# A hybrid decoder step on one core: key copies, gated-row copies, sample exponentials and the scores of two narrow steps moved

## What is computed

```python
def diff_attn_core(q, k, v, qpos, kpos, rel_bias, lam):
    s = jnp.einsum('bqhmd,bkhmd->bhmqk', q, k2) * (QK_HEAD_DIM ** -0.5)
    dist = qpos[:, None] - kpos[None, :]
    s = jnp.where(dist >= 0, s + bias[None, :, None], NEG_INF)
    p = jax.nn.softmax(s, axis=-1)
    a = p[:, :, 0] - lam * p[:, :, 1]
    return jnp.einsum('bhqk,bkhd->bqhd', a, v)
# prompt: causal over its own 1024 keys; sample: over 8 cached pages and its own 8 keys
# o_b = rmsnorm(attention output per head); o_a = u * (tril(W) LayerNorm(v) + b)
# mix = concat(o_b, o_a) @ w_out; x = x + rmsnorm(mix); then ConvFFN: w_up, conv 3, silu(g) * u, w_down
```

## Time and profile before

| | us |
|---|---|
| median of three runs | 1390.12 |
| the profiled execution | 1389.97 |
| its span | 1388.2 |
| TensorE busy | 1360.4 (98%) |
| VectorE busy | 700.8 (50%) |
| ScalarE busy | 460.8 (33%) |
| GpSimd busy | 169.9 (12%) |

### The profile page before, as it was taken

One profiled execution on the slowest core, in us unless ns is written; L12 is line 12 of the kernel. 1 busy time (PEld: TensorE's weight loads), 2 busy tenths in 40 slices (PEclk: granted clock), 3 DMA queues, 4 the chain that ended last, 5 costly groups with the idle time before them and its releaser, 6 DMA issues.

```text
span 1388.2 us, 22368 instructions
## 1 busy us (share of the span) xinstructions
PE 1360.4 (98%) x8646; PEld 1222.2 (88%) x8646; DVE 700.8 (50%) x1169; ACT 460.8 (33%) x780; POOL 169.9 (12%) x322
## 2 busy tenths in 40 slices
PE   7999999989999999999999999999999999999997
PEld 6999999956667788899898989898989898999986
DVE  5333412166778565454546463636454545364555
ACT  5321012055657543343131313231323232322332
POOL 2254000021222221120000000000000000000003
PEclk9999999999999999999999999999999999999999
DMA  7202123256664624132020111111110202020117
GB/s 264 63 31 65 31 69 106 73 175 183 198 192 159 214 90 136 46 106 76 16 76 15 60 30 60 30 60 30 44 46 17 74 15 76 15 67 23 46 31 133
DMA packets 93290, 112.65 MB, mean 81 GB/s; under 512 B 6429, under 2 KB 65222, under 8 KB 93222
## 3 DMA queue, kind: packets, MB, share of 16 engines
q1 hardware_dynamic: 89845, 103.60, 23.7%
q0 software_dynamic: 1136, 4.06, 1.8%
q10 hardware_dynamic: 2240, 4.06, 0.8%
HBM read 96.76 MB, written 14.69 MB: 80 GB/s over the span
## 4 chain that ended last, share of the span: by engine, by line
PE 92%; DVE 2%; issue 2%; ACT 1%; POOL 1%; DMA 1%; SPq 0%; ACTq 0%; DVEq 0%; POOLq 0%
PE PS L2271 37%; PE PS L1996 17%; PE PS L2335 16%; PE PS L2214 7%; PE PS L2082 2%; PE PS L2044 2%; PE PS L2350 2%; PE PS L2365 2%; PE PS L2105 2%; PE PS L2151 1%; PE PS L2128 1%; PE PS L2070 1%; PE PS L1982 1%; PE PS L2206 1%; DMA x_in<-in_x_prompt_dram 1%
## 5 line engine op out<-in xcount | busy, mean ns | idle before, releaser
L2271 PE MATMUL PS<-act_lo,wu_hi 128*128 128x364 f32 (+1 forms) x1056 | 346.4, 328 | 0.0
L2271 PE MATMUL PS<-act_hi,wu_hi 128*128 128x364 f32 (+1 forms) x1056 | 346.0, 328 | 0.2 <-DVE wu_lo L1807 0.2
L2271 PE MATMUL PS<-act_hi,wu_lo 128*128 128x364 f32 (+1 forms) x1056 | 346.0, 328 | 0.0
L2271 PEld LDWEIGHTS PS<-act_hi,wu_hi 128*128 128x128 f32 x1056 | 198.5, 188 | 1.0 <-DVE wu_lo L1807 0.5
L2271 PEld LDWEIGHTS PS<-act_lo,wu_hi 128*128 128x128 f32 x1056 | 198.1, 188 | 0.4
L2271 PEld LDWEIGHTS PS<-act_hi,wu_lo 128*128 128x128 f32 x1056 | 198.4, 188 | 0.0
L1793 DVE TENSOR_TENSOR y_acc<-y_acc,PS 128x512 f32<-128x512 f32 x162 | 111.2, 686 | 115.9 <-PE PS L2335 115.9
L2335 PE MATMUL PS<-wd_hi,g_hi 128*128 128x512 f32 x324 | 130.1, 401 | 0.0
L2335 PE MATMUL PS<-wd_lo,g_hi 128*128 128x512 f32 x324 | 128.0, 395 | 0.0
L2335 PE MATMUL PS<-wd_hi,g_lo 128*128 128x512 f32 x288 | 114.0, 396 | 0.0
L1198 ACT CAST g_hi<-conv 128x1088 fp32r<-128x1088 f32 x21 | 23.1, 1102 | 245.8 <-PE PS L2335 189.7
(11 more groups left out here) (269 smaller groups left out, 2379.7 us busy)
## 6 DMA issues: line engine op xcount, KB each, us to landing
wu_raw<-in_w_up_dram SPq DMA_DIRECT2D x44, 512.0 KB, 3.9
vpage<-in_cache_v_dram SPq DMA_DIRECT2D x64, 256.0 KB, 3.0
kpage<-in_cache_k_dram SPq DMA_DIRECT2D x60, 256.0 KB, 3.0
wd_raw<-in_w_down_dram SPq DMA_DIRECT2D x22, 512.0 KB, 5.3
w_raw<-in_w_in_dram SPq DMA_DIRECT2D x20, 512.0 KB, 4.8
wo_raw<-in_w_out_dram SPq DMA_DIRECT2D x8, 512.0 KB, 5.5
x_res<-in_x_prompt_dram SPq DMA_DIRECT2D x8, 512.0 KB, 4.3
out_dram<-x_mid SPq DMA_DIRECT2D x8, 512.0 KB, 2.9
```

The lines of the kernel that those rows point to most:

```text
L2271: mm = nc.tensor.matmul(PS[:, 3 * half + c, 0:kept(c)], a[:, half, k, :], b[:, k, KEPT[c]], start=(j == 0), stop=(j == len(parts) - 1))
```

## The change

Six edits, all in the order of work in attention and none in what is computed:

- In step 1 VectorE copies key 3 ahead of mix(0), and in step 2 key 5 right behind mix(1). The maximum of the sample group's own scores (`own_max`) moves from step 0 to behind mix(0).
- `out_norm` runs ahead of the mix in steps 3, 4, 12 and 20 (`norm_first`).
- GpSimd copies the gated rows one by one, each behind the factor of steps 0 to 3, in place of all four ahead of step 0's factor and without the wait for six maxima.
- The sample exponentials of steps 3, 7, 11, 15 and 19 run in the next step on ScalarE: behind `out_square` and ahead of `take_turned` for the first half of a pair, behind `take_turned` for the second, with the partial exponential.
- The scores of steps 9 and 17 (two key blocks) are computed right behind those of steps 8 and 16 (one key block), in the same bank from column 128 on (`JOINED`).
- `near_max` of steps 8 and 16 waits for the scores of the next step too.

SyncE's list is not touched.

```diff
--- before.py
+++ after.py
@@ -484,12 +484,26 @@
 
         return last_user(i, 1 if second_bank(i) else 0) < i - 1
 
+    JOINED = (QB, 2 * QB)
+
+    def bank_user(i, b):
+
+        return last_user(i - 1 if i - 1 in JOINED else i, b)
+
+    def norm_first(i):
+
+        return i == 3 or (i >= 3 and early(i) and wide_step(i))
+
+    def late_exponent(i):
+
+        return i % 4 == 3 and i < 2 * QB + 4
+
     def wides_before(i):
         return sum(wide_step(j) for j in range(i))
 
     def score_from(i):
 
-        return P if width(i) == 5 else 512 if second_bank(i) else 0
+        return P if width(i) == 5 or i - 1 in JOINED else 512 if second_bank(i) else 0
 
     def score_cols(i, m):
 
@@ -1067,8 +1081,13 @@
         for i in range(NSTEP):
             if i >= 3:
                 out_square(i - 3)
+            if i >= 1 and late_exponent(i - 1) and i % 8 == 4:
+                smp_exponent((i - 1) // 8, 0)
             if i >= 2:
                 take_turned(i - 2)
+            if i >= 1 and late_exponent(i - 1) and i % 8 == 0:
+                smp_exponent((i - 1) // 8, 1)
+                part_exponent((i - 1) // 8)
             if i == NSTEP - 3:
                 split_w_out(4)
             if i == NSTEP - 2:
@@ -1089,7 +1108,7 @@
                 own_exponent()
             if i in SMP_STEP:
                 smp_take(SMP_STEP.index(i))
-            if i % 4 == 3 and i < NSTEP - 1:
+            if i % 4 == 3 and i < NSTEP - 1 and not late_exponent(i):
                 smp_exponent(i // 8, i // 4 % 2)
                 if i % 8 == 7:
                     part_exponent(i // 8)
@@ -1317,9 +1336,6 @@
             pool.wait_ge(krow_stored[i], 16 * ((STEPS + 1 - i) // 2))
         nc.gpsimd.memset(bias_sb[:, :, 0:2 * P], 0.0).then_inc(bias_zero, 1)
         pool.wait_ge(job_ready, len(jobs))
-        pool.wait_ge(nmax_ready, 2 * 3)
-        for g in range(AG):
-            nc.gpsimd.tensor_copy(res[:, 4 + g, 0:NTOK], uT[:, g, :]).then_inc(gated_kept, 1)
 
         for i in range(NSTEP):
             c = slice(i % 4, i % 4 + 1)
@@ -1329,6 +1345,8 @@
             nc.gpsimd.tensor_tensor(o_rstd[:, c], o_mean[:, c], neg_half, ALU.pow).then_inc(pool_step, 1)
             own_step(pool, pool_step)
             nc.gpsimd.tensor_tensor(o_fac[:, c], o_rstd[:, c], precip[:, i % 4, 0:1], ALU.mult).then_inc(ofac_ready, 1)
+            if i < AG:
+                nc.gpsimd.tensor_copy(res[:, 4 + i, 0:NTOK], uT[:, i, :]).then_inc(gated_kept, 1)
 
         pool.wait_ge(sscore_ready, 4 * NB)
         pool.wait_ge(turn_ready, turns_before(NSTEP))
@@ -1477,7 +1495,7 @@
 
         def near_max(i, m):
             h, w = i // QB, P * width(i)
-            dve.wait_ge(score_ready, 2 * i + m + 1)
+            dve.wait_ge(score_ready, 2 * (i + 1 if i in JOINED else i) + m + 1)
             if wide_step(i):
                 dve.wait_ge(far_ready, 2 * wides_before(i) + m + 1)
             c = edge(i) if wide_step(i) else 0
@@ -1533,6 +1551,8 @@
                 c0 = P + DS * (6 - 2 * pr)
                 nc.vector.tensor_tensor(own[:, pr, :], PS[:, OWN_BANK, NS * pr:NS * pr + NS], smp_bias[:, c0:c0 + NS],
                                         ALU.subtract).then_inc(own_biased, 1)
+
+        def own_max():
             dve.wait_ge(own_biased, NB // 2)
             nc.vector.tensor_reduce(part_nmax[:, :, 2], own[:], AX.X, ALU.max, negate=True).then_inc(omax_ready, 1)
 
@@ -1675,8 +1695,16 @@
                     far_max(i, 1)
                 else:
                     near_max(i, 0)
+            if i == 1:
+                take_keys(3)
+            if norm_first(i):
+                out_norm(i - 3)
             if i >= 1:
                 mix(i - 1)
+            if i == 1:
+                own_max()
+            if i == 2:
+                take_keys(5)
             if i in ZERO_STEP and i >= 28:
                 zero_values()
             if i == NSTEP - 3:
@@ -1686,14 +1714,14 @@
             for m in range(2):
                 if wide_step(i) and not early(i):
                     far_max(i, m)
-                if i >= 3 and m == 0 and wide_step(i):
+                if i >= 3 and m == 0 and wide_step(i) and not norm_first(i):
                     out_norm(i - 3)
                 if i >= 2 and (wide_step(i) or not early(i) or m == 1):
                     near_max(i, m)
-                if i >= 3 and m == 0 and not wide_step(i):
+                if i >= 3 and m == 0 and not wide_step(i) and not norm_first(i):
                     out_norm(i - 3)
             for n in keys_of(i):
-                if n % 2 == 1:
+                if n % 2 == 1 and n not in (3, 5):
                     take_keys(n)
             if i == 0:
                 own_softmax()
@@ -2036,7 +2064,7 @@
             qs = slice(NS + P * (n - 1), NS + P * n)
             parts = [(0, edge(i)), (edge(i), w)] if wide_step(i) else [(0, w)]
             for j, (c, e) in enumerate(parts):
-                user = last_user(i, 1 if second_bank(i) else j)
+                user = bank_user(i, 1 if second_bank(i) else j)
                 if user >= 0:
                     pe.wait_ge(prob_ready, 2 * user + 2)
                 for m in range(2):
@@ -2157,8 +2185,10 @@
             mm.then_inc(pv_ready, 1)
 
         for i in range(NSTEP):
-            if i >= 2:
+            if i >= 2 and i - 1 not in JOINED:
                 scores(i)
+            if i in JOINED:
+                scores(i + 1)
             if i % OB == 3 and i >= 7:
                 turn_out((i - 7) // OB)
             for n in keys_of(i):
```

## The result

The changed kernel takes 1406.17 us (median of four runs, 1405.18 to 1406.31) against 1389.92 us for the kernel before: ratio 1.0119, 95% interval 1.0107 to 1.0131, so 16.3 us slower. The profiled execution took 1405.18 us with a span of 1403.5.

A forecast was written before the change was run, and what follows sets the result against it. TensorE's own work, gaps and half-clock stretches bound the kernel. Key 20's delay 13.0, clock 1.2, step 16 -1.0 and steps 12 and 20 +0.5 sum to +13.7 us on 1389.97: 1403.7 us, range 1400 to 1407.

The forecast's parts named there:

- The wait and its queue: SyncE's first value load waits for the fourth gated copy, to 313.2 us; key unit 4, queued behind, lands at 328.7.
- first stall: Step 7: TensorE waits 11.4 us for key 16, from 317.3 to 328.7.
- The second stall: Step 9: TensorE waits 2 to 4 us more for key 20, which stands at 342.0, 13.0 us later than before.
- The clock term: After the second stall TensorE may stay at 1.2 GHz for 3 to 4 us; +1.2 us taken, 0 to 1.7 possible.
- Rival C: Clock stays at 1.2 GHz through steps 9 and 10, adding 4 to 5 us: 1408 us; 7%.
- Part 1 and 2's gains: Key copies ahead of mixes and gated rows copied singly shrink the gaps of steps 1 and 3; 1.0 us left after step 5.
- Part 3: out_norm ahead of mix in steps 3, 4, 12 and 20; +0.25 us each in 12 and 20, from 0.4 gain to 0.7 loss.
- part 4: Later sample exponentials and paired scores of steps 8/9 and 16/17 remove the 1.03 us gap; counted in step 16 as -1.04 us.
- Rival A: Only local gains show, 2.6 us, if the fourth copy is done by about 301 us: 1387.4 us; 4%.
- Rival B: One stall only: the load queue issues faster, at 0.94 us, so key unit 5 is in time; +10.3 us, 1400.3 us; 8%.

The follow-up runs named there:

- e2_one_by_one_only: The kernel before with the one edit that GpSimd copies the gated rows one by one; 1407.90 us, 1.0127 of the kernel before.
- e5_values_behind: The changed kernel with SyncE issuing key units 4 and 5 ahead of values 0 and 1; 1385.25 us, 0.9970 of the kernel before.
- e7_norm_3_4: e3_block_early with out_norm ahead of the mix in steps 3 and 4 alone; 1385.61 us, 0.9974 of the kernel before.
- e11_not_late: e5_values_behind with all sample exponentials back in steps 3, 7, 11, 15 and 19; 1391.93 us, 1.0018 of the kernel before.
- e10_no_pairs: e5_values_behind with the scores of steps 9 and 17 back in their own steps; 1385.81 us, 0.9980 of the kernel before.
- e3_block_early: The changed kernel with the four gated copies as one block ahead of all factors, without the wait for maxima; 1385.89 us, 0.9975 of the kernel before.
- e9_stall_step9: The changed kernel with SyncE issuing key unit 4 ahead of values 0, for the first pair of sequences; 1401.98 us, 1.0093 of the kernel before.
- e6_no_pairs_late: e3_block_early without the paired scores and without the later sample exponentials; 1390.47 us, 1.0010 of the kernel before.
- e4_unit5_first: The changed kernel with SyncE issuing key unit 5 ahead of values 1, for the first pair of sequences; 1398.46 us, 1.0068 of the kernel before.

## Why the prediction was right, and where it was off

- **The wait and its queue** carried the prediction, and hold to a few tenths: first value load 313.2 predicted and 313.31 measured, key 16 at 328.7 and 328.86, first stall 11.4 and 11.22 us, key 20 at 342.0 and 342.32. e2_one_by_one_only shows that this edit alone is the loss, e5_values_behind that it is the queue and not the copies.
- **The second stall**, 2 to 4 us predicted, is 2.83; that the clock loss after the first stall hides in it holds too, since key 20 stands where the loads put it.
- **The clock term was mis-sized.** Part "The clock" took +1.2 us (0 to 1.7) from stretches of 3 to 4 us. It is 4.72 us: the half clock lasted 10.2 us. The step that failed is the use of the first projections and of the end of attention as the nearest rows: there wide products or `smp_weigh` came soon. Rival C, put at 7%, is what happened in steps 9 and 10; its "against" (the clock came back amid such work at 482) misread the row, since the work there was wide products and then `smp_weigh`'s 64 matmuls (from 481.80), amid which it came back in the changed kernel too. The 4 to 5 us priced for C is the measured size. The rule cited beside it from the Trainium skill (TensorE: Matmul & The Clock Gate, "Part 4: PE-mode transpose"), that transposes don't count as activity the way matmuls do, doesn't explain it: behind the second stall the key transposes end at about 343.9, and nearly all of the remaining 9 us at half clock are matmuls; behind the stall of step 7 key transposes come first as well, and the clock was back within 3.5 to 4.5 us.
- **The end of attention** was taken as fixed. In the profile of after the half-clock stretch there is missing, about -1.5 us in span. The errors partly cancel: 13.31 + 4.72 - 0.17 - 0.93 - 0.18 - 1.5 = 15.3 us, where 13.0 + 1.2 - 1.0 + 0.5 = 13.7 was predicted. The medians are 16.3 us apart. The three unprofiled runs are 1 us above the profiled one and have a mean granted clock of 0.990 against 0.992, so they spent longer at half clock; where, no trace shows.
- **The range held partly by luck.** With 4.72 us in place of 1.2 the prediction's own sum is 17.2 us, 1407.2, above its upper end of 1407. The time came out inside since the end of attention (-1.5 us) and steps 12 and 20 (-0.35 in place of +0.5) happened to be better than forecast. The mechanism of the two stalls isn't luck.
- **Part 1 and 2's gains**: step 1's gap 1.01 to 0.31 (0.7 predicted), step 3's gone. At step 5 TensorE is 0.85 us ahead (305.10 to 304.25), 1.0 predicted.
- **Part 3** was predicted at +0.25 us each for steps 12 and 20. Measured are -0.17 and -0.18, but by e7_norm_3_4 these belong to part 4, and the norm first is worth nothing with the later exponentials and costs 0.7 us without them (e11_not_late). The upper loss named, 0.7 us, was the right size for a case that the change doesn't contain.
- **Part 4**: step 16's gap gave 0.93 us (17.86 to 16.93), 1.04 predicted. The cause was given to two edits, and only one has it (e10_no_pairs).
- **Rival A**'s price, 2.6 us of local gains, is near what e3_block_early (3.0 us) and e5_values_behind (4.0 us by medians, 0.30%) bring once the queue is not blocked. In the profile of the second, TensorE is 3.4 us ahead at step 27 (438.54 to 435.17), and about 1.5 us more is the half clock at the end of attention, which it doesn't have. Its condition, the fourth copy done by about 301 us, is the one that e3_block_early meets.
- **Rival B**'s sum has a slip: from 322.4 to the end of unit 5 it is 16 issues and not 20. At 0.94 us each they end near 337.4, the last load lands near 340, and with TensorE there at 338.1 a second wait of some 2 us would have been left. The queue kept its pace (8.03 us for 8 value issues), so B didn't come up.

## What to carry to other kernels

Before spreading a producer's work over later steps, list all that waits for its last part, and then all that is queued behind each waiter: here one wait of a load queue, ahead of values that were wanted some 20 us later, held the loads wanted first. Either keep the last piece early, or put the wait behind the urgent loads; both recover the gain. And price a stall of TensorE not by its length alone but with the clock behind it: a wait of 2.83 us was followed by 4.72 us lost at half clock, and taking it away brought 6.6.

## What was not expected of the hardware

- After a stall in step 9, TensorE at 0.50 clock (1.2 GHz) for 10.2 us (changed kernel), 10.0 us (e2_one_by_one_only) and 11.4 us (e9_stall_step9) while it was busy throughout with eight transposes and then 64-, 256- and 128-column matmuls; after a stall in front of step 7's work, 3.5 to 4.5 us.
- The fall after the short second stall came 0.3 us after TensorE had resumed (342.32, 0.50 from 342.6 on), not in the stall.
- The same 1.3 us gap at the end of attention brought a half-clock stretch in some profiles (3.4 us in the kernel before, e2_one_by_one_only and e3_block_early, 6.8 us in e6_no_pairs_late and e11_not_late) and none in others (the changed kernel, e4_unit5_first, e5_values_behind). What decides it isn't shown.
